# A mixture-of-experts step in which h rides in each slot's result: a fourth weight place, another issue order, a final stage without TensorE

## The reference

```python
    h = x + mixed.astype(x.dtype)
    hn = _rmsnorm(h, p['g_ffn']).reshape(b * l, D_MODEL)
    h = h + _hier_moe(hn, p).reshape(b, l, D_MODEL)
...
# _hier_moe: 4 groups x 8 experts, the best group, the best 2 experts in it
        a = xb @ p['moe_w_gate'][e]
        v = xb @ p['moe_w_up'][e]
        return (jax.nn.silu(a) * v) @ p['moe_w_down'][e]
...
y_prompt = _rmsnorm(yp, g_final)
```

## Time and profile before

| what | value |
|---|---|
| median of 3 runs | 1182.9 us (1175.76, 1182.9, 1187.05) |
| profiled execution | 1188.38 us |
| its span, first to last instruction | 1186.5 us |
| PE busy in the span | 1103.2 us (93%) |
| DVE, ACT, POOL busy | 442.5, 250.1, 113.8 us |
| moved by DMA | 271.84 MB, mean 229 GB/s |
| mean granted TensorE clock | 0.965 |

### The profile page before, as it was taken

One profiled execution on the slowest core, in us unless ns is written; L12 is line 12 of the kernel. 1 busy time (PEld: TensorE's weight loads), 2 busy tenths in 40 slices (PEclk: granted clock), 3 DMA queues, 4 the chain that ended last, 5 costly groups with the idle time before them and its releaser, 6 DMA issues.

```text
span 1186.5 us, 17459 instructions
## 1 busy us (share of the span) xinstructions
PE 1103.2 (93%) x7006; PEld 538.5 (45%) x7006; DVE 442.5 (37%) x1051; ACT 250.1 (21%) x489; POOL 113.8 (10%) x202
## 2 busy tenths in 40 slices
PE   7999999999998999999999999989999998988645
PEld 4666665767754654555453333333333332322211
DVE  4799989360177743232541101110011010100107
ACT  4300112113544853221210000000000000000017
POOL 0000000000072000000410010001001000100015
PEclk9999999999997989998979999999999999999968
DMA  8121123013003021103959999999999999999758
GB/s 310 50 84 38 55 67 44 1 42 96 20 2 147 1 110 73 41 20 136 363 179 342 414 416 356 411 414 416 387 413 399 414 413 412 413 412 414 315 202 323
DMA packets 73778, 271.84 MB, mean 229 GB/s; under 512 B 10784, under 2 KB 15712, under 8 KB 65632
## 3 DMA queue, kind: packets, MB, share of 16 engines
q1 hardware_dynamic: 67200, 252.47, 55.4%
q0 software_dynamic: 6048, 17.83, 3.9%
q10 hardware_dynamic: 448, 0.40, 0.1%
HBM read 251.18 MB, written 23.55 MB: 232 GB/s over the span
## 4 chain that ended last, share of the span: by engine, by line
PE 60%; DVE 17%; DMA 8%; SPq 7%; ACT 4%; issue 3%; POOL 0%; POOLq 0%; ACTq 0%; DVEq 0%
PE psA L1157 17%; PE psB L1186 9%; DVE psC L1716 7%; SPq L579 6%; PE psA L1007 5%; PE psB L1007 4%; DMA arena<-in_w_up 3%; PE psA L684 3%; PE psC L808 3%; PE psB L684 2%; DMA arena<-in_w_down 2%; PE psA L827 2%; PE psC L1142 1%; DMA arena<-hn_rows,ints 1%; DVE arena L1716 1%
## 5 line engine op out<-in xcount | busy, mean ns | idle before, releaser
L1157 PE MATMUL psA<-arena 128*32 128x512 f32 x2688 | 299.8, 601 | 23.8 <-DMA arena<-in_w_up 22.0
L1157 PEld LDWEIGHTS psA<-arena 128*32 128x32 f32 x2688 | 87.4, 111 | 218.5 <-issue 215.3
L1186 PE MATMUL psB<-arena 128*32 128x512 f32 x1344 | 152.0, 602 | 8.6 <-DMA arena<-in_w_down 8.6
L2165 DVE TENSOR_TENSOR arena<-psA,arena 128x512 f32<-128x512 f32 x21 | 14.5, 692 | 321.2 <-ACT arena L1531 321.2
L684 PE MATMUL psA<-arena 128*128 128x360 f32 (+1 forms) x384 | 120.8, 474 | 7.9 <-DVE arena L1590 7.9
L684 PE MATMUL psB<-arena 128*128 128x360 f32 (+1 forms) x384 | 118.9, 468 | 0.0
L684 PEld LDWEIGHTS psA<-arena 128*128 128x128 f32 x384 | 73.4, 192 | 52.1 <-DMA arena<-in_w_cm 7.9
L684 PEld LDWEIGHTS psB<-arena 128*128 128x128 f32 x384 | 72.8, 190 | 43.5 <-issue 0.5
L1716 DVE SCALAR_TENSOR_TENSOR psC<-arena,params,psC 128x1024 f32<-128x1024 f32 x70 | 89.9, 1284 | 0.0
L1186 PEld LDWEIGHTS psB<-arena 128*32 128x32 f32 x1344 | 42.7, 111 | 102.1 <-issue 99.7
L1531 ACT ACTIVATE arena<-psA 128x512 f32<-128x512 f32 x21 | 12.5, 597 | 311.4 <-PE psA L1157 311.4
(11 more groups left out here) (438 smaller groups left out, 1191.4 us busy)
## 6 DMA issues: line engine op xcount, KB each, us to landing
arena<-in_w_gate SPq DMA_DIRECT2D x128, 512.0 KB, 13.2
arena<-in_w_up SPq DMA_DIRECT2D x128, 512.0 KB, 16.3
arena<-in_w_down SPq DMA_DIRECT2D x64, 1024.0 KB, 15.3
arena<-expert_rows SPq DMA_DIRECT2D x16, 512.0 KB, 10.0
arena<-in_w_cm SPq DMA_DIRECT2D x15, 512.0 KB, 3.5
arena<-in_xT SPq DMA_DIRECT2D x8, 544.0 KB, 8.5
arena<-in_w_out SPq DMA_DIRECT2D x1, 4096.0 KB, 12.7
arena<-in_x_rows SPq DMA_DIRECT2D x8, 512.0 KB, 7.4
```

Source lines behind the costliest of these rows:

```text
L1157: mm = te.matmul(psA[tile, at:at + FF], xgT[:, k, tile], w[o % RG][:, k, :], start=(k == 0), stop=(k == KT - 1))
L1186: mm = te.matmul(psB[tile, n * 512:(n + 1) * 512], hT[:, k * P + c * TW:k * P + c * TW + TW], w, start=(k == 0), stop=(k == 3))
```

## The change

- **h in the slot's result.** Each slot's result becomes `2 * gate * down + rms * xg`, where `rms * xg` is h again. ACT writes `rms * xg` into `orow` (`rows_scaled`), and one DVE operation of 128 x 1024 adds the scaled PSUM rows (`rows_added`), in place of the two copies. The sum of a token's two rows is then 2h + 2 moe, and the final norm uses 4 eps. For this, a small table of pairs (2 * gate, rms) goes to HBM (`gates_and_rms`), written by ACT once DVE has the gates, and POOL gathers 128 pairs of 8 bytes for each quad (`gather_scales`). The gates are computed in quad 0 and no longer in quad 1.
- **Buffers.** `xg` has three buffers, `orow` one. h's SBUF (`arena2`) becomes a fourth place for gate and up.
- **Weight DMAs.** An expert's parts are now gate first half, gate second half, up first half, up second half, each one DMA of 1 MB with rows of 8 KB. gate_up does all gate matmuls first, and silu starts after them. A table, `DOWN_BEFORE`, sets where each down matrix stands between the gate and up loads, and `VISIT` is another order. Stores of hn rows move from SP's queue to ACT's.
- **The end.** No PE, no POOL and no scaling by ACT: DVE adds the two rows, the rest is as before.

```diff
-RG, RD, GC, DC = 3, 2, 4, 2
+RG, RD, GC, DC = 4, 2, 4, 2
+DOWN_BEFORE = [3, 4, 7, 7, 8, 10, 10, 11, 12, 12, 13, 16, 17, 17, 18, 19, 21, 21, 22, 24, 24, 25, 26, 27, 28, 29, 29, 30,
+               30, 32, 32, 32]
+GU_PART = [(m, slice(h * 2 * KT // GC, (h + 1) * 2 * KT // GC)) for m in range(2) for h in range(GC // 2)]
...
-                for w, src in ((wg[r], a["w_gate"]), (wu[r], a["w_up"])):
-                    sp.dma_start(w[:, ks, :], src[ds(e, 1), :, :].rearrange("o (p k) n -> (o p) k n", k=KT)[:, ks, :]
-                                 ).then_inc(s_wgu[r][c], 16)
+                r, (m, ks) = n % RG, GU_PART[c]
+                w, src = ((wg[r], a["w_gate"]), (wu[r], a["w_up"]))[m]
+                sp.dma_start(w[:, ks, :], src[ds(e, 1), :, :].rearrange("o (p k) n -> (o p) k n", k=KT)[:, ks, :]
+                             ).then_inc(s_wgu[r][c], 16)
...
                 if n == E - 1:
-                    sp.wait_ge(m_gu, GC * LAST_Q[E - 3] + GC)
-                elif n >= 2 * RD:
+                    sp.wait_ge(m_gu, GC * LAST_Q[FREED] + GC)
+                    sp.wait_ge(m_dn, DC * FIRST_Q[E - 3] + c + 1)
+                elif n >= RD + 2:
                     sp.wait_ge(m_dn, DC * LAST_Q[n - RD] + c + 1)
                 elif n >= RD:
-                    sp.wait_ge(m_dn, DC * LAST_Q[RD - 1] + DC)
+                    sp.wait_ge(m_dn, DC * LAST_Q[1] + DC)
...
+            for n in range(4, E + 1):
+                for d in range(2, E):
+                    if DOWN_BEFORE[d] == n:
+                        e = expert(d)
+                        for c in range(DC):
+                            down_in(d, e, c)
+                if n < E:
+                    e = expert(n)
                     for c in range(GC):
-                        for n, e in zip([n for n in NEW[q] if n > 2], ahead):
-                            gate_up_in(n, e, c)
...
+            def rows_scaled(q):
+
+                ac.wait_ge(s_tab, 16 * (q + 1))
+                if q:
+                    ac.wait_ge(s_os, 16 * q)
+                ac.activation(orow, xg[q % 3], ACT.Identity, scale=scales[q % 2][:, 1:2]).then_inc(m_dnA, 1)
...
+                if q == 0:
+                    ac.wait_ge(rt_dve, RT["table"])
+                    ac.dma_start(tab_dram.rearrange("(p n) c -> p (n c)", p=P), gate_table.rearrange("p k i c -> p (k i c)")
+                                 ).then_inc(s_hst[0], 16)
...
+                ve.scalar_tensor_tensor(out=orow, in0=psB[:, 0:D], scalar=scales[q % 2][:, 0:1], in1=orow,
+                                        op0=ALU.mult, op1=ALU.add).then_inc(m_dnD, 1)
...
+            gather(0)
+            gather(1)
+            gather_scales(0)
+            gather_scales(1)
+            gather(2)
             for q in range(NQ):
-                if q + 1 < NQ:
-                    gather(q + 1)
-                if q:
-                    scatter(q - 1)
-            scatter(NQ - 1)
+                scatter(q)
+                if q + 2 < NQ:
+                    gather_scales(q + 2)
+                if q + 3 < NQ:
+                    gather(q + 3)
```

More of the change, by code:

```diff
@@ L97 @@
       "dest6": 146,
-      "dest7": 186, "slots": 197, "diag": 229, "dm": 198, "d4": 199, "spill": 206}
+      "dest7": 186, "slots": 197, "dm": 198, "d4": 199, "spill": 206, "rows": 227, "table": 234}
 class Steps:
@@ L195, in encoder_step @@
         a3 = Arena(arena3)
-        wd = [a3.take(4 * D).rearrange("p (k n) -> p k n", k=4) for _ in range(RD)]
-        wd_first = [mix[:, :, n * 4 * P:(n + 1) * 4 * P] for n in range(RD)]
+        wd = [a3.take(4 * D).rearrange("p (k n) -> p k n", k=4) for _ in range(2)]
+        wd_first = [mix[:, :, n * 4 * P:(n + 1) * 4 * P] for n in range(2)]
         a4 = Arena(arena4)
@@ L245, in encoder_step @@
         m4 = Arena(arena4)
-        xg = m4.take(D)
+        xg0 = m4.take(D)
         xgT = m4.take(D).rearrange("p (k n) -> p k n", k=KT)
         actg, hmid, hT = (m4.take(FF) for _ in range(3))
[L249 to L259, removed]
+        orow = m4.take(D)
+        xg = [xg0, m4.take(D), arena2[:, (NT - 1) * D:NT * D]]
+        FREED = E - RG
+        freed_at = 0
+        wd_last = arena1[:, freed_at:freed_at + 4 * D].rearrange("p (k n) -> p k n", k=4)
+        gfin_row = freed_at // D + 4
+        gfin = arena1[:, gfin_row * D:(gfin_row + 1) * D]
+        rows = [arena1[:, n * D:(n + 1) * D] for n in range(24) if n != gfin_row]
+        og = [rows[2 * i:2 * i + 2] for i in range(NT)]
         yrow = [og[i][0] for i in range(NT)]
@@ L303, in encoder_step @@
         slotm = rt.take(BLOCKS)
+        tile_of, row_of = scaled, slotc
+        gate_table = rt.take(2 * NT * 2).rearrange("p (k i c) -> p k i c", k=2, c=2)
+        scales = [rt.take(2) for _ in range(2)]
+        eps4 = rt.take(1)
         pairs = negmask
@@ new lines, in _ @@
+            firsts = [expert(n) for n in range(4)]
+            for n in range(2):
+                for c in range(GC):
+                    gate_up_in(n, firsts[n], c)
+            sp.wait_ge(*wo_act.at(3, "hn"))
+            for c in range(2):
+                gate_up_in(2, firsts[2], c)
+            sp.wait_ge(wo_pe, 4)
+            for c in range(DC):
+                down_in(0, firsts[0], c)
+            sp.wait_ge(*wo_act.at(5, "hn"))
+            gate_up_in(2, firsts[2], 2)
+            sp.wait_ge(wo_pe, 8)
@@ L620, in _ @@
+            for c in range(DC):
+                down_in(1, firsts[1], c)
+            sp.wait_ge(*wo_act.at(7, "hn"))
+            gate_up_in(2, firsts[2], 3)
             sp.wait_ge(wo_pe, NT)
             for c in range(GC):
-                gate_up_in(2, firsts[2], c)
-            sp.wait_ge(*wo_dve.at(NT - 1, "add"))
-            sp.dma_start(hres[0:TS, NT - 1, 512:D], last_h[TS:2 * TS]).then_inc(s_xtok[1], 16)
-            for q in range(1, NQ + 1):
-                if q < NQ:
-                    ahead = [expert(n) for n in NEW[q] if n > 2]
-                    for c in range(GC):
-                        for n, e in zip([n for n in NEW[q] if n > 2], ahead):
-                            gate_up_in(n, e, c)
-                if q >= 2:
-                    behind = [expert(n) for n in NEW[q - 1]]
-                    for c in range(DC):
-                        for n, e in zip(NEW[q - 1], behind):
-                            down_in(n, e, c)
@@ L1504, in _ @@
                     ac.wait_ge(tr_pe, NT + 1)
[L1505 removed]
+                    ac.activation(ssum[:, i:i + 1], psB[:, 512:513], ACT.Sqrt, scale=1.0 / D, bias=col("eps")
                                   ).then_inc(*wo_act.of("rms"))
@@ L2152, in gates @@
                 linkr(ve.tensor_tensor(gate[1], gate[0], gs, ALU.mult))
+                ve.tensor_scalar(eps4, col("eps"), 4.0, None, ALU.mult)
+                for k in range(2):
+                    ve.tensor_scalar(gate_table[:, k, :, 0], gate[k], 2.0, None, ALU.mult)
+                    last = ve.tensor_copy(gate_table[:, k, :, 1], ssum)
+                linkr(last, "table")
             def rows_moved(q):
```

238 lines of the change are left out of this document (108 added, 130 removed).

## The result

The changed kernel takes 1197.61 us in the median of 4 runs (1195.43 to 1200.05), the kernel before beside it 1180.95 (1175.76 to 1187.05): a ratio of 1.0126, 95% interval 1.0083 to 1.017. It is slower, by about as much as was forecast (1199). The profiled execution has a span of 1195.3 us, 8.8 more than that of before, where the sum gave 16.

What follows compares the result with a forecast made beforehand. PE and DMA were both taken as near their limits, the row round trip as equally tight. +9 start, +25 loop, -15 tail, -3 final stage gave +16, so 1199 us on the median's scale; range up to 1222, down into the cheap pairs.

Steps and rivals of the forecast that it cites:

- Start, +9 forecast: Before the loop: gather(2) goes out behind both gathers of pairs, so turn_rows(2) starts at 657.7 instead of 648.58, +9 us.
- Loop, +25 forecast: Eighteen quads: a longer row round trip makes PE wait 2.6 us a quad, period 25.4, 457 us against 432.
- I charge each pair one turn of a weight row: Loop, pairs between scatter and gather: eight per engine at 0.32 us each, 2.5 us added to the round trip.
- rival of cheap pairs: Loop: an engine's eight pairs pass in one turn, 0.3 us, and bytes set the period; 1168 us, 27% chance.
- (a): The start: first pairs are computed, stored and fetched before quad 2's rows; POOL's second gather of pairs charged 1.3 us; +9 us.
- (b): The loop: scatter 0.59 us later and pairs 2.5 us in the queue lengthen the round trip to 17.1 us; +25 us.
- one sentence on down(2): Loop loads: SP still stops at down(2), behind expert 6's loads, until down(0) is over, delayed further by the start; no size.
- signs that the prediction named: If right: row waits about 2.6 us, trip near 15, turn_rows(2) near 658, hardly any up/down waits, loop DMA below 400 GB/s.
- Tail, -15 forecast: From turn_rows(20) to the last product: weights no longer late except 3.6 us, so 42.8 us instead of 57.9.
- final stage, -3 forecast: After the last product: scaling, addition and PE's products removed, 0.6 us multiply-add added; -3 us, between +0.6 and -8.
- The dry ring: Loop: while PE waits, SP's stream stops and the gather meets an emptier queue; 24.3 us a quad, 1179 us, 15% chance.
- Dear pairs: Loop: pairs cost as much as rows, 3.8 us for eight, a period of 26.7; 1223 us, 8% chance.

Runs made afterwards that it cites:

- pairs behind: Changed kernel, but in the loop POOL gathers the rows of quad q+3 ahead of the pairs of quad q+2: 1197.19 us, ratio to before 1.0107.
- rows off the path: Changed kernel with quad 2's rows gathered before the first pairs and, in the loop, rows gathered ahead of the scatter once ACT has scaled: 1177.55 us, ratio 0.9951.
- the last run: Changed kernel with three places for gate and up, four for down, and another load order; POOL's order unchanged: 1180.16 us, ratio 0.9978.

## Why the prediction was right, and where it was not

The direction and the size held: 1.26% slower (0.83 to 1.7%) for 1.4% forecast. Of the four terms, two were right and two missed in opposite directions, and that the total came so near is in part luck: span against span the sum was 7 us too high (16 for 8.8), and the medians lie as far apart as forecast only because the two profiled executions stood so differently to theirs. How much an execution varies is seen ahead of the mixture: its first turn_rows starts at 616.95 in the changed kernel and anywhere from 611.74 to 618.15 in the ten runs above.

**Start, +9 forecast, +13.4 measured.** The mechanism was right: 10.5 of the 13.4 are the wait for gather(2), and the run with quad 2's rows first takes that wait away and 8.6 us with it. The other 4.8 stay there and are none of this term: most of it is a mixture that began 1.4 us later, which lies within the spread just named, and a gate_up(0) of 16.74 us for 13.94, whose cause is open. The forecast for gather(2) itself was too early. The store went out at 639.22 and not at 637.6, since the move of quad 1's rows ended 2.8 us later than before (637.48 for 634.65), while the small operations and ACT's handover took 1.2 less than I put. It landed after 6.5 us for the 5 I took (645.75), and the first pairs after 6.7 for 6, with two handovers of 0.3 between. Of the 4.4 us by which the term was too small, that is 4.3. Behind the stall, 72 matmuls ran 2.6 us slower, which the loop's figure holds.

**Loop, +25 forecast, +13.9 measured.** This is the step that failed: "I charge each pair one turn of a weight row". Eight pairs are one packet, which the packet counts show, and moving them away shortened the trip by 0.9 us, not 2.5. So the rival of cheap pairs was right on their price in the queue. By the rule of the Trainium skill (page "DMA: Bandwidth & Descriptors", section "SWDGE vs HWDGE vs iDMA") a packet holds up to 64 descriptors; this case's 32 packets a quad agree with it. What the sum of the loop left out is POOL's issue of the pairs, 1.33 us a quad, which (a) had charged once and (b) did not. The scatter's later start, 0.59 in the sum, was 0.1: down's end to the scatter's issue is 1.70 us (696.56 to 698.26) where it was 1.60. The multiply-add does take 0.59 us longer (1.28 for 0.69), but the scatter goes out 0.3 us behind DVE's end where it was 0.8, in every quad; that POOL now waits for one engine and not two may be why, and was not tried. The trip came to 13.9 us, under the 14.9 forecast for it (17.1 less 2.2).

Yet the rival's time, 1168, did not follow, since it took bytes for the next limit. The next limit was SP's stream, stopped at down. I had priced the fourth place and the new order of loads at nothing, as weight waits "which the row trip now covers anyway", with one sentence on down(2); it is the part I did not see. Taking away the row waits, in whole or in part (pairs behind, rows of 4 KB, rows off the path), brings the waits for down up from 11.8 us to 15.9, 23.2 and 20.4 in the loop. Taking away the down waits by other places and another order lets the row waits fall too, to 9.3 us, and both away give 23.7 us a quad. So the two stand in for each other in part. Taken out of the changed kernel, the row waits alone are worth 7.0 us of the loop (rows off the path, 24.39 a quad), the down waits alone 15.4 (the last run, 23.92, a little less than before's 24.0), both 19.2.

Which of the two makes the +13.9 against the kernel before is not shown. That kernel had two places for down as well and no wait for down in the loop, so the two places by themselves are not the cause; the new order in SP's stream is the likely one, since another table with the same two places took 9.6 us off the loop. No run has the table or `VISIT` of before in the changed kernel, or the four places with its table. By the waits, rows rose by 15.0 us and weights fell by 2.7, from 14.5 for up to 11.8 for down.

Of the signs that the prediction named, one came as said, DMA below 400 GB/s in the loop (382). The row wait (0.85 us a quad for 2.6) and the trip (13.9 for 15) were smaller, turn_rows(2) later (662 for 658), and waits for down came where hardly any were expected.

**Tail, -15 forecast, -15.9 measured; final stage, -3 forecast, -2.6 measured.** Both right in size. The last quads wait 2.48 and 1.45 us for weights where they waited 16 in all; the rest is PE's busy time, 37.95 us for 41.79 at a granted clock of 1.00 for 0.94. What brings the weights early is not settled: with down on ACT's queue the tail is 8 us longer without the fourth gate and up place, but with three places and four for down it is 38.5. The parts of the final stage were not tried one by one.

The dry ring, the rival of no change, failed in its reason: in the five quads behind the start whose stretch has 331 to 362 GB/s the trip is 12.6 to 14.9 us, hardly shorter than the median of all. Dear pairs are excluded by the packet count.

## What to carry to other kernels

Before a small transfer is put into a queue, ask what stands behind it and when that is needed: here one gather's place was 13 us, as much as the whole difference between the kernels, while the pairs ahead of it took one packet per engine. When two waits end within a microsecond of each other, removing one shows the other; run each removal alone and both together before a cause is named. Where one engine issues all loads, its own waits show at which buffer it stops, and so where to try another order or more places; they do not say what that is worth, since the better table made SP stop longer at down. Here another table gave 6 us, and two places for down in place of one for gate and up, with a table for them, 14.

## What the runs showed of the hardware

- Behind waits of PE of 3.83 and 4.38 us, 64 matmuls took 9.47 and 9.05 us instead of 7.07 (granted clock 0.74 and 0.78 over them); behind one of 2.40 us they took 7.07 at a granted clock of 1.00, but 9.72 us behind one of 2.73 in the run with the pairs behind and 8.77 behind one of 2.35 in the run with rows of 4 KB.
- Gathered rows of 8 bytes travelled eight to a packet (32 packets for 128 rows, of which I read 16 as the ones that every indirect DMA has beside its rows), rows of 4 KB one to a packet (144 for 128 rows).
- With down on ACT's queue, and so a third busy queue, the row trip had a median of 17.1 us instead of 13.9.
- In stretches of about a quad at a full share, DMA moved 416 to 422 GB/s with all weights in rows of 8 KB, and 410 to 415 in the run with gate and up in rows of 4 KB.
